# A first block in another order: memory attention ahead, decays inside the local attention, memory keys scaled at eviction

## The reference, cut to what matters

```python
h = rms_norm(x, norm_g)
p = h @ w_in                     # r, k, v, w, a, z_a | q, sk, sv, z_b | xq, z_c | gates
y_a = rwkv7_mix(...) * silu(z_a)                      # recurrence over time, 8 heads of 64
y_b = sliding_window_sink_attn(p_q, p_sk, p_sv, ...) * silu(z_b)   # window 128, 8 heads, 2 key heads
y_c = memory_cross_attn(p_xq, mem, ...) * silu(z_c)   # 4 heads of 128 over 256 memory tokens
merged = sum of sigmoid(gate_i) * (y_i @ w_proj_i)
x = x + merged @ w_out

def memory_cross_attn(q, mem, mem_norm_g, w_mem_kv, xq_g, xk_g):
    q = rms_norm(q per head, xq_g)
    kv = rms_norm(mem, mem_norm_g) @ w_mem_kv
    km, vm = kv[..., :X_WIDTH], kv[..., X_WIDTH:]
    km = rms_norm(km per head, xk_g)
    ...softmax(q km) vm

def rwkv7_mix(...):              # before the scan
    r, k, v, lw, la = token_shift_mix(p, mu)          # u + (previous token - u) * mu
    decay = exp(-exp(-softplus(-(w0 + tanh(lw) @ w2)) - 0.5))
    a = sigmoid(a0 + la @ a2)
    kk = k * k_k, normed per head;  k = k * (1 + (a - 1) * k_a)
```

## Time and profile before

| | |
|---|---|
| runs | 1932.92 us median of 3 (1932.4 to 1935.56) |
| the profiled execution | 1931.05 us, its span 1928.9 us |
| PE | busy 1783.4 us, 92% of the span |
| PE weight load | 909.8 us, 47% |
| VectorE (DVE) | 712.4 us, 37% |
| ScalarE (ACT) | 422.1 us, 22% |
| GpSimd (POOL) | 136.2 us, 7% |
| granted TensorE clock, mean | 0.968 of full |
| DMA | 119.75 MB, 62 GB/s on average |

### The profile page before, as it was taken

The page is one execution under the profiler, slowest core; times in us unless marked ns, Lnnn a source line. Parts: engine busy times, 40 slices in busy tenths (PEclk is TensorE's granted clock), DMA queues, the critical chain, the costliest instruction groups (busy, mean ns, idle before and its releaser), DMA issues.

```text
span 1928.9 us, 20481 instructions
## 1 busy us (share of the span) xinstructions
PE 1783.4 (92%) x8040; PEld 909.8 (47%) x8040; DVE 712.4 (37%) x1456; ACT 422.1 (22%) x800; POOL 136.2 (7%) x124
## 2 busy tenths in 40 slices
PE   5998789996799999999999979999999999999997
PEld 3643334452355555544454457644644444444443
DVE  3006434445533333322438988521424222221012
ACT  4022533343211111020215322400301111111000
POOL 0002120000000100000006700000000000000001
PEclk8999899998899999999999979999999999999998
DMA  4311011110001111112221112122012222221121
GB/s 181 107 66 44 33 55 44 55 44 33 33 34 35 34 34 34 34 55 95 76 76 66 66 55 66 45 77 72 27 66 77 76 76 77 76 76 66 66 87 65
DMA packets 34159, 119.75 MB, mean 62 GB/s; under 512 B 3792, under 2 KB 4048, under 8 KB 33680
## 3 DMA queue, kind: packets, MB, share of 16 engines
q1 hardware_dynamic: 32976, 113.79, 17.4%
q10 hardware_dynamic: 864, 3.35, 0.4%
q0 software_dynamic: 224, 1.31, 0.2%
HBM read 116.34 MB, written 2.10 MB: 61 GB/s over the span
## 4 chain that ended last, share of the span: by engine, by line
PE 78%; DVE 12%; issue 5%; ACT 4%; DMA 1%; POOL 0%; ACTq 0%; DVEq 0%; POOLq 0%
PE bank L462 55%; PE vpair L582 3%; PE bank L888 3%; DVE arena L1291 3%; PE bank L478 2%; PE bank L512 2%; PE opair L606 2%; DVE tmp L1282 2%; PE abank L697 2%; DVE arena L1707 2%; PE abank L555 1%; PE vpair L697 1%; DVE max L1706 1%; PE bank L487 1%; PE vpair L566 1%
## 5 line engine op out<-in xcount | busy, mean ns | idle before, releaser
L462 PE MATMUL bank<-h,ring 128*128 128x512 f32 x1840 | 835.0, 605 | 24.3 <-ACT tmp L997 14.6
L462 PEld LDWEIGHTS bank<-h,ring 128*128 128x128 f32 x1840 | 346.3, 193 | 437.2 <-issue 404.0
L462 PE MATMUL bank<-arena,ring 128*128 128x512 f32 (+1 forms) x992 | 406.0, 563 | 14.0 <-ACT arena L980 8.2
L462 PEld LDWEIGHTS bank<-arena,ring 128*128 128x128 f32 x992 | 187.8, 194 | 209.8 <-issue 184.9
L1291 DVE SCALAR_TENSOR_TENSOR x<-bank,x 128x512 f32<-128x512 f32 x32 | 22.1, 692 | 260.0 <-PE bank L462 216.7
L1291 DVE SCALAR_TENSOR_TENSOR arena<-arena,cols 128x512 f32<-128x512 f32 x125 | 94.0, 752 | 4.4
L1282 DVE TENSOR_TENSOR arena<-arena,vpair 128x256 f32<-128x256 f32 x87 | 36.6, 421 | 156.1 <-PE vpair L697 109.9
L980 ACT ACTIVATE arena<-bank 128x512 f32<-128x512 f32 (+1 forms) x67 | 34.7, 518 | 269.2 <-PE bank L462 211.1
L1285 DVE TENSOR_SCALAR arena<-arena,cols 128x512 f32<-128x512 f32 x24 | 13.1, 546 | 206.8 <-ACT arena L1246 206.6
L582 PE MATMUL vpair<-arena 128*128 128x256 f32 (+4 forms) x224 | 72.1, 427 | 7.5 <-issue 4.3
L555 PE MATMUL abank<-sq,cst 128*128 128x512 f32 (+1 forms) x58 | 33.6, 720 | 44.8 <-ACT sq L952 37.5
(11 more groups left out here) (194 smaller groups left out, 1564.0 us busy)
## 6 DMA issues: line engine op xcount, KB each, us to landing
ring<-weights SPq DMA_DIRECT2D x201, 512.0 KB, 3.2
ring<-weights SPq DMA_DIRECT2D x16, 256.0 KB, 2.9
x<-xt SPq DMA_DIRECT2D x4, 512.0 KB, 7.6
out<-h SPq DMA_DIRECT2D x8, 256.0 KB, 2.1
cst<-cst_in ACTq DMA_DIRECT2D x1, 1504.0 KB, 14.2
arena<-memt ACTq DMA_DIRECT2D x1, 1024.0 KB, 7.8
arena<-mem2t POOLq DMA_DIRECT2D x1, 1024.0 KB, 5.1
tmp<-pos ACTq DMA_DIRECT2D x1, 256.0 KB, 10.3
```

The lines of the kernel that those rows point to most:

```text
L462: last = mm(o[:, 0:n], weight(), src, start=c == 0, stop=c == len(srcs) - 1)
```

## The change

All of it is in the first block; the weights in memory and the launch are the same.

1. **Front.** The first two memory-key groups (`memory_keys(0)`) run on the memory times its gain, not yet divided by its norm (`memg`); VectorE multiplies with the reciprocal norm as it reads the bank (`scaled_keys`), and then scales the `memg` tiles in place for the value groups, each once `memory_keys(1)` has used it. The squares are added over tiles on VectorE (`add_square`), so that each norm takes one ones-multiply instead of eight. The angles move behind the application of the x norm. SyncE issues two weight panels ahead of x, ScalarE the position, constant and lora loads behind its memory squares.
2. **Order of the groups.** km, vm, xq, yc silu, memq, skn, sv, lora tile; then, as fill of the attention, yb silu, k, r and v in turn, ya silu.
3. **Attention.** Memory jobs first, then window jobs. The rotations (steps 1 to 6), the norm of k and the first decay (step 13) and the other decays (16, 19, 22) are inserted (`inject` on PE, `before` on ScalarE, `after` on VectorE). In the rotations' steps VectorE releases the scores' bank first (`free_scores`).
4. **Gates.** All eight output tiles (`GATES`) go beside the recurrence, 12 pairs in a step instead of 9. Scratch: the six decay buffers `E` lie on `xq` and `km` instead of the softmax buffers; the arena grows by one tile for `lwa`.

```diff
-        stage("attention operands", *[A8] * (8 + 10 + 8))
-        stage("recurrence operands", *[A8] * 17)
-        stage("gates early", *[A8, V4, A8, V4] * len(EARLY))
-        stage("gates late", *[A8, V4, A8, V4] * len(LATE))
+        GATES = (4, 5, 0, 1, 2, 3, 6, 7)
+        stage("front operands", ("dve", 2 * KD), ("dve", 2 * KD), *[A8] * (4 + 4 + 4 + 4 + 2 + 1))
+        stage("attention fill", *[A8] * (4 + 4 + 8 + 4))
+        stage("gates", *[A8, V4, A8, V4] * len(GATES))
...
+            def memory_keys(g):
+
+                o = dense_bank()
+                for n in range(2):
+                    for c in range(KD):
+                        if g == 0 and n == 0:
+                            next_h()
+                        last = mm(o[:, n * M:(n + 1) * M], weight(), memg[:, c, :], start=c == 0, stop=c == KD - 1)
+                        if g == 1 and n == 1 and c < KD - 1:
+                            h_used.inc(last)
+                end_group(last)
...
+            memory_keys(0)
             pe.wait_ge(ones_in.sem, 16)
...
+            single("a", con("ones"), mem_squares[:, 0, :], M)
+            memory_keys(1)
             for n in range(4):
...
+                for _ in dense_tokens_pairs(memg, 2, normed=n == 0):
+                    pass
+                if n == 1:
+                    norm_total()
             dense_normed()
...
+            inject = {}
+            for i in range(4):
+                inject[1 + i] = lambda i=i: rotate_query(i)
+                inject[DECAY_AT[i]] = lambda i=i: decay_sums(i)
+                inject[DECAY_AT[i] + 2] = lambda i=i: bonus_sum(i)
+            for s in range(2):
+                inject[5 + s] = lambda s=s: rotate_key(s)
...
+            inject[7] = rotated
...
+            inject[KK_AT] = first_decay
+            pe.wait_ge(wa2_in.sem, 16)
+            attention(memory_jobs() + window_jobs(), work, inject=inject)
             finish(work)
...
-                    fill(work)
+                    if it == 0:
+                        pe.wait_ge(o_read.sem, gates_from)
+                    fill(work, 2)
...
+            for i in range(KD):
+                act.wait_ge(x_in[i // 2].sem, 16)
+                do(fn(slot(i), x[:, i, :], ACT.Square), square_ready)
+            norm_rinv(1, 1.0 / D, col("eps6"))
+            for n in range(4):
+                copy_dense(vm[:, :, tok(n)], dense_in()[:, 0:M].rearrange("p (s d) -> p s d", s=2))
...
+            before = {KK_AT: kk_squares}
+            for i in range(4):
+                before[DECAY_AT[i] + 1] = lambda i=i: decay_tanh(i)
+                before[DECAY_AT[i] + 2] = lambda i=i: decay_exps(i)
...
+            after = {}
+            for i in range(4):
+                after[1 + i] = lambda i=i: rope_between(lambda: rope(memq[:, i, :], memq[:, i, :]))
+                after[DECAY_AT[i] + 1] = lambda i=i: decay_sums(i)
+                after[DECAY_AT[i] + 2] = lambda i=i: decay_apply(i)
...
             for p in range(NPANEL):
+                if p == 2:
+                    for i in range(4):
+                        sp.dma_start(x[:, 2 * i:2 * i + 2, :], xt[:, 2 * i:2 * i + 2, :]).then_inc(x_in[i].sem, 16)
```

More of the change, by code:

```diff
@@ L317, in stage_groups @@
             return groups[start[name]:start[after]]
-        RECUR = stage_groups("recurrence operands", "gates early")
-        GEARLY = stage_groups("gates early", "gates late")
+        FILL1 = stage_groups("attention fill", "gates")
         CROSSKV = [(who, n or KD) for who, n in stage_groups("cross kv", "w_out_2")]
-        GLATE = stage_groups("gates late", "gates a")
+        GATED = stage_groups("gates", "gates a")
         nblocks = sum(n for _, n in groups)
@@ L405, in cross_jobs @@
             return jobs
-        v_before = []
+        v_of_jobs = []
+        KK_AT = 13
+        DECAY_AT = (13, 16, 19, 22)
+        MIXED = [(lwa, 12)] + [(k[:, i, :], 4 + i) for i in range(4)] + [
+            (dst[:, i, :], m + i) for i in range(4) for dst, m in ((r, 0), (v, 8))]
+        GATE_PAIRS = 12
         SPLIT = 14
@@ L545, in take_pair, with norm_sums @@
                 return vpair if kind == "v" else opair
-            def norm_sums(ones, norms, tiles, n=T):
+            def norm_sums(ones, norms, tiles, n=T, first=0):
                 for i in range(norms):
@@ L568, in _, with attention @@
             att = {"p": 0, "pt": 0}
-            def attention(jobs, work=iter(()), fills=even_fills):
+            def attention(jobs, work=iter(()), fills=even_fills, inject={}):
                 n = len(jobs)
-                v_before.append(state["v"])
+                v_of = []
+                v_of_jobs.append(v_of)
                 for i in range(n + 3):
@@ L620, in _ @@
             dense_normed()
-            for n in range(4):
+            dense(h)
+            norm_sums(con("ones"), 4, 1, M)
+            for n in range(2):
                 dense(h)
-            dense_tokens(h, NT)
-            for n in range(4):
-                dense(h)
-            pe.wait_ge(cst_in.sem, 16)
-            work = stream([hs] * 8)
-            norm_sums(con("head_ones"), 4, 1)
-            fill(work, 8)
-            norm_sums(con("head_ones"), 1, 1)
-            fill(work, 4)
@@ L632, in _ @@
-            for i in range(4):
+            work = stream([hs] * 9)
+            fill(work, 4)
+            for i in range(2):
+                norm_sums(con("ones"), 2, 1, first=2 * i)
+                fill(work, 2)
+            finish(work)
+            pe.wait_ge(cst_in.sem, 16)
+            work = dense_tokens_pairs(h, NT)
+            for i in range(5):
+                fill(work, 2)
+                norm_sums(con("head_ones"), 1, 1, first=i)
+            finish(work)
+            dense(h)
@@ L633, in _, with rotate_query, rotate_key @@
+            work = stream([hs] * 20)
+            pe.wait_ge(norm_applied.sem, 2 + 4 + 4)
+            def rotate_query(i):
                 pe.wait_ge(rope_in.sem, i + 1)
                 single("v", con("rot"), memq[:, i, :])
-            fill(work, 4)
-            pe.wait_ge(rope_in.sem, 5)
-            for s in range(2):
+            def rotate_key(s):
+                pe.wait_ge(rope_in.sem, 5)
                 single("v", con(f"dup{s}"), skn)
                 single("v", con(f"rotdup{s}"), skn)
-            fill(work, 4)
@@ L662, in _ @@
+            inject[7] = rotated
+            assert KK_AT == DECAY_AT[0]
+            inject[KK_AT] = first_decay
+            pe.wait_ge(wa2_in.sem, 16)
+            attention(memory_jobs() + window_jobs(), work, inject=inject)
             finish(work)
-            work = stream([hs, ybs, hs, ycs] * len(LATE))
+            ybs, ycs = ([y[:, c, :] for c in range(4)] for y in (yb, yc))
+            work = stream([hs, ybs, hs, ycs] * len(GATES))
+            gates_from = state["o"]
             n_ml = n_xx = 0
@@ L942, in a_in, with norm_squares @@
                 return bank[4 + (st["a"] - 1) % 2]
-            def norms(srcs, tiles, ln_scale, eps, out_bias="zero", n=T, scales=None, refined=False, after=None, preload=False):
+            def norm_squares(srcs, n=T, scales=None, after=None):
                 act.wait_ge(norm_applied.sem, st["norm"])
-                if preload:
-                    nc.scalar.preload_act_table_set("natural_log_exp_and_others")
                 for i, s in enumerate(srcs):
@@ L962, in norms @@
                 st["norm"] += cnt
+            def norms(srcs, tiles, ln_scale, eps, out_bias="zero", n=T, scales=None, refined=False, after=None, preload=False):
+                if preload:
+                    act.wait_ge(norm_applied.sem, st["norm"])
+                    nc.scalar.preload_act_table_set("natural_log_exp_and_others")
+                norm_squares(srcs, n, scales, after)
+                norm_rinv(len(srcs) // tiles, ln_scale, eps, out_bias, n, refined)
             def silu_in(dst):
@@ L1783, in do @@
                 pool.wait_ge(sig.sem, sig.n)
-            dst = [y[:, n] for y in (yb, yc, ya) for n in range(4)]
+            dst = [y[:, n] for y in (yc, yb, ya) for n in range(4)]
             for n in range(12):
```

283 lines of the change are left out of this document (158 added, 125 removed).

## The result

The changed kernel takes **1852.71 us** (median of 4 runs, 1851.45 to 1854.25); the kernel before, run beside it, 1934.24 (1932.4 to 1935.66). The ratio is 0.9579, 95% interval [0.9563, 0.9596]: faster by 81.5 us. The forecast was 1858, 5.3 more. The profiled execution took 1854.25 us, its span is 1852.4 (before 1928.9), its mean clock 0.982 (before 0.968).

What follows compares the result with a forecast made beforehand. PE, busy 92% of the span, was taken as the bound, leaving its idle time and slow clock to win. Attention and front -114.6, gates +41.4, idle given back -1: -74.2 from 1931.05, plus 1.9 for the median, 1858; range 1834 to 1886.

Steps and rivals of the forecast that it cites:

- First scores: Front of the first block: PE starts at 9.5 us and reaches the first scores at 168.1, before 245.1.
- The charge for the clock: Front: 0.38 us of slower PE clock for each us of new wait, 4.1 for 10.9 us of waits.
- Attention: First block's attention with rotations and decays: 215.1 work, 18.7 waits and 7.1 clock make 240.9 us.
- in all 11: Attention: PE's waits for the four decays, at score and dense banks and the first decay's norm, sum to 11 us.
- clock 7.1: Attention: slower PE clock behind 18.7 us of waits costs 7.1 us.
- Recurrence: First block's recurrence: 48 gate blocks moved in add 41.4 us, less perhaps 1 of idle time; some 339 us long.
- "-1" given back: Recurrence: two more gate pairs per step beside VectorE waits save perhaps 1 of 17.4 idle us; bounds -5 and +5.
- the 46 that I had named as a sign of being wrong: Recurrence: growth by more than 46 us would show the prediction wrong.
- stay dear: Rival, attention: decays still cost PE 27.7 us of waits instead of 11; time 1890; chance 0.10.
- in series: Rival, attention: scores, softmax, rotations and decays wait for each other, 92 us instead of 18.7; time 1959; chance 0.02.
- The start was won: Front: memory lands at 9.0 us; the rival, landing at about 20.5, adds 11, time 1869, chance 0.03.
- The table loads: Switches ahead of PE waits: priced at the trace's 1.28 us; the skill's drain would add 15.4, giving 1873.

Runs made afterwards that it cites:

- experiment 9: Changed kernel with value copies 0 and 1 ahead of the x norm and ScalarE's Sin moved behind the silu inputs; 1847.32 us.
- experiment 5: Changed kernel with the window query norms run in pairs as soon as two tiles are there; 1849.83 us.
- experiment 7: Changed kernel with decays and k norms again after the attention, beside the gates of two tiles, and 9 gate pairs per recurrence step; 1887.55 us.
- experiment 2: Changed kernel with SyncE issuing the four x loads ahead of the first weight panel, as before; 1856.01 us.
- experiment 3: Changed kernel with ScalarE copying value groups 0 and 1 before the Ln and Exp of the x norm; 1851.06 us.

## Why the prediction was right, point by point

Its sum was -74.2 on the span; the profile has -76.5. The parts:

- **First scores, 168.1 forecast, 170.67 measured.** The waits were right: 4.7, 2.6, 3.6 against 4.57, 2.49, 4.30, half a us more in sum. The charge for the clock, 4.1 at 0.38 for each us of wait, was nearly right for what lay behind the waits: the values lost 2.9 behind the 4.57 (10.18 against 7.31), the seven groups behind 102.53 lost 1.8. The term that was missing is the start: 2.2 us were lost on the first keys (9.28 against 7.07), which I had priced at full speed. Other work came out 0.7 shorter.
- **Attention, 240.9 forecast, 233.4 measured.** The entry was right (6.4 against 6.54), the absence of waits at the other rotations too; the dense bank behind the entry cost 0.47 instead of 1.3. The terms that failed are "in all 11" for the decays and "clock 7.1". The decays' waits are 7.9: decay 3 costs nothing instead of 1.0, decay 2 1.2 instead of 1.8, decay 1 2.2 instead of 2.5, the first 4.57 in all instead of 5.7. The clock: 233.4 less the 215.1 of work and 14.95 of waits leaves 3.3. Of it 2.6 are the three rows right behind the entry (2.05, 1.91 and 2.56 us, where such rows take 1.02, 1.03 and 1.88 later); the second half, which holds the 7.9 us of short waits, has a granted clock of 1.00. The rate of 0.38 fits the wait of 6.54; applying it to the short waits too was the error. Nor do short waits always cost nothing: behind the same wait (2.16, at 334.0) experiment 9 has a clock of 0.66 from 334 to 339, and its attention is 1.5 longer.
- **Recurrence, +40.4 forecast, +45.3 measured.** The "-1" given back failed: PE's idle time is 17.2 us, before 17.4, and nearly all waits have their old lengths. Against +41.4 for the blocks PE's busy time grew by 45.5. The blocks were priced right and the rest is clock, as experiment 5 shows, whose recurrence is the same code. Columns as in the earlier trace rows, of the changed kernel and of experiment 5:

```profile
404.05:748.14 344.09, 326.85 (x3803) 194.43 (x3801) 107.40 (x224) 43.03 (x90) 33.95 (x42) 0.98 0.12 40
399.44:739.28 339.84, 322.61 (x3802) 191.91 (x3801) 107.42 (x224) 43.04 (x90) 33.95 (x42) 0.99 0.12 40
```

  There PE is busy for 41.2 more than before (281.4) and the recurrence is 41.1 longer. In sixteenths of the recurrence the changed kernel has a clock below 1.00 in three (0.92, 0.92, 0.84), experiment 5 in the last alone (0.92). So +45.3, close to the 46 that I had named as a sign of being wrong, holds 4.2 us of clock that came with this execution.
- These three misses (+2.6, -7.5, +4.9) cancel, so that the end of the recurrence, 748.14, met 748.2 by luck as much as by right. The mechanisms were right, the clock was mis-sized with both signs: put at nothing at the start and in the recurrence, too dear in the attention.
- **Afterwards.** What lies behind the recurrence (the end of the first block and the second) took 1104.3 us, before 1106.6. No edit touches it, and experiments 5 and 7 have 1106.4 and 1106.5, so these 2.3 us are scatter. And the profiled execution lies 1.5 above its median, not 1.9 below, as I had carried over from before: 3.4. With 0.3 between span and time this makes 6.0: the sum and the 1.9 give 1858.7, which the prediction wrote as 1858, and from there the miss is 5.3.
- **The rivals.** The decays did not stay dear (7.9 us of waits, that case had 27.7), and not in series: waits of 14.95 in the attention, far from the 73 of that case. The start was won (experiment 2 shows on what it hangs). By experiment 7 the decays cost 53 us outside the jobs beyond the two gate tiles beside them (94.8 - 41.5), inside 18.5.
- **The table loads.** The Trainium skill (ScalarE: Activation LUTs, What ACT_TABLE_LOAD costs) would have had 15.4 us more in this walk, by my estimate from its drain of 1.38 us. The trace stays against it: in experiment 5 a load of 1.28 has its activation 0.01 behind (156.09, then 157.38).
- **VectorE beside GpSimd.** Adding nothing was right. At the rotations VectorE's rows take their 0.69 us, since it mostly waits while GpSimd works (198.56 to 201.39). Beside the pairs at the end of the attention two rows grew, to 1.38 instead of 0.48 at 387.37 and to 3.09 instead of 2.15 at 393.36, and PE did not wait.

## What to carry to other kernels

Where engines take their work in order, look at the order before the load: edits that only changed it (a bank's read ahead of a norm, a Sin behind the silu inputs, norms in pairs, banks read one job sooner) took 23.8 us from a kernel whose VectorE and ScalarE are busy for 39 and 23% of the span. A part that slow engines bound (the decays) can be cut in pieces and laid into a part that leaves them room, with its PE work moved to where PE is the bound: here it cost 18.5 us inside the attention and 41.1 to 45.3 in the recurrence, in place of 94.8. When a wait is taken away, look for the next in line, as Sin stood behind experiment 3. And judge small edits by the marks of the traces, not by medians alone: stretches that no edit touched moved by up to 4 us.

## What the runs showed of the hardware that I had not expected

**PE starts slowly, and the granted clock does not tell it.** The same 32 records of the first keys took 9.28 us here, 8.55 in experiment 2, 10.04 in experiment 3; the next 32 took 7.07 each time. Windows of 1 us of the changed kernel (length, PE busy with records, granted clock, DMA share, GB/s):

```profile
11.00:12.00 1.00, 1.00 (x4) 1.00 1.05 418
...
16.00:17.00 1.00, 1.00 (x6) 1.00 1.26 487
17.00:18.00 1.00, 1.00 (x7) 1.00 0.99 421
```

```profile
22.00:23.00 1.00, 1.00 (x4) 1.00 0.00 0
...
26.00:27.00 1.00, 1.00 (x6) 1.00 0.00 0
```

The Trainium skill (TensorE: Matmul & The Clock Gate, Part 1) has 1.2 GHz as the level of an idle array; the pace agrees with it, only the column does not show it before the first change of level.

**A wait of 4.57 brought the clock down for longer than it lasted itself.** Behind it, in the same columns:

```profile
37.00:38.00 1.00, 0.00 (x0) 0.83 0.00 0
...
41.00:42.00 1.00, 1.00 (x6) 0.50 0.00 0
...
46.00:47.00 1.00, 1.00 (x12) 1.00 0.68 127
```

It fell to the level of 1.2 GHz during the wait and stayed there for some 5.8 us of work, at half pace. Behind the same wait of 4.57 these two groups took 8.97 to 10.21 us in seven kernels (7.31 at full clock), so that one wait had a price of 1.7 to 2.9 us from run to run. Such scatter can explain why medians moved by less or more than the waits that an edit took away; edits are judged here by the marks of the trace as well.
